# Moving the first of four merges to an earlier tick in a hand-ordered attention-layer kernel

## The reference, cut to what matters

```python
outs, lses = [], []
for g, (win, dil) in enumerate(zip(DSW_WINDOWS, DSW_DILATIONS)):
    sl = slice(g * DSW_HEADS_PER_GROUP, (g + 1) * DSW_HEADS_PER_GROUP)
    o_g, lse_g = dilated_window_attention(qa[:, :, sl], ka[:, :, sl], va[:, :, sl], win, dil)
    outs.append(o_g)
    lses.append(lse_g)
alpha = jax.nn.softmax(jnp.stack(lses), axis=0)
ya = jnp.sum(alpha[..., None] * jnp.stack(outs).astype(jnp.float32), axis=0)
ya = ya.astype(x.dtype).reshape(B, S, DSW_OUT_WIDTH) * jax.nn.silu(za)
pa = ya @ w_proj_a
...
yd = differential_attention(qd, kd, vd, lam)
yd = rms_norm(yd, diff_subln) * (1.0 - lambda_init)
yd = yd.reshape(B, S, DIFF_V_WIDTH) * jax.nn.silu(zd)
pb = yd @ w_proj_b
ga, gb = jnp.split(jax.nn.sigmoid(gm), 2, axis=-1)
y = (ga * pa + gb * pb) @ w_out
```

## Time and profile before

| | |
|---|---|
| time, three executions | 837.82, 837.94, 839.5 us (median 837.94) |
| profiled execution, first to last instruction (the only time shown of it) | 835.3 us |
| TensorE matmul busy | 791.2 us, 95% |
| VectorE, ScalarE, GpSimd busy | 462.2, 360.6, 464.1 us |
| mean granted TensorE clock | 0.979 of full speed |

### The profile page before, as it was taken

The page is one execution under the profiler, slowest core; times in us unless marked ns, Lnnn a source line. Parts: engine busy times, 40 slices in busy tenths (PEclk is TensorE's granted clock), DMA queues, the critical chain, the costliest instruction groups (busy, mean ns, idle before and its releaser), DMA issues.

```text
span 835.3 us, 12656 instructions
## 1 busy us (share of the span) xinstructions
PE 791.2 (95%) x4590; PEld 663.8 (79%) x4590; DVE 462.2 (55%) x715; ACT 360.6 (43%) x777; POOL 464.1 (56%) x616
## 2 busy tenths in 40 slices
PE   3989899998899999999979998998999999999997
PEld 2867798887688888888768787777887778888897
DVE  5855653647646363334686597678666653113632
ACT  6455445533354544434434545455466442323310
POOL 4742545546566573458485586779266276637200
PEclk9889999998999999999989999999999999999999
DMA  9943323385233333243522332243112123324431
GB/s 320 338 141 110 109 73 95 96 284 158 92 97 93 120 101 102 85 143 102 145 75 77 99 92 90 77 123 95 51 63 70 46 75 102 102 76 144 159 102 51
DMA packets 87076, 95.39 MB, mean 114 GB/s; under 512 B 9405, under 2 KB 78310, under 8 KB 87014
## 3 DMA queue, kind: packets, MB, share of 16 engines
q1 hardware_dynamic: 86944, 94.56, 36.6%
q10 hardware_dynamic: 70, 0.02, 0.0%
HBM read 78.53 MB, written 5.54 MB: 101 GB/s over the span
## 4 chain that ended last, share of the span: by engine, by line
PE 67%; DVE 14%; issue 7%; ACT 4%; POOL 3%; DMA 3%; SPq 2%; DVEq 0%; POOLq 0%; ACTq 0%
PE proj L1731 48%; PE proj L1850 4%; PE sums L1654 3%; PE turned L1622 2%; DVE dstat L1346 2%; POOL w_lo L787 2%; PE score L1604 2%; PE score L1570 2%; PE proj L1780 2%; PE sums L1656 2%; ACT probs L1031 2%; DMA rope_s<-rope_x 1%; DVE dstat L1362 1%; DVE at_lo L1369 1%; ACT junk L1063 1%
## 5 line engine op out<-in xcount | busy, mean ns | idle before, releaser
L787 POOL TENSOR_TENSOR w_lo<-raw,w_hi 128x256 fp32r<-128x256 f32 x376 | 299.7, 829 | 209.3 <-ACT w_hi L907 209.3
L1731 PE MATMUL proj<-h_hi,w_hi 128*128 128x512 f32 x560 | 231.5, 413 | 0.0
L1731 PE MATMUL proj<-h_hi,w_lo 128*128 128x512 f32 x560 | 221.6, 396 | 0.0
L1731 PE MATMUL proj<-h_lo,w_hi 128*128 128x512 f32 x560 | 220.1, 393 | 0.0
L1731 PEld LDWEIGHTS proj<-h_hi,w_hi 128*128 128x128 f32 x560 | 106.6, 190 | 30.3 <-issue 8.9
L1731 PEld LDWEIGHTS proj<-h_hi,w_lo 128*128 128x128 f32 x560 | 106.2, 190 | 24.0
L1731 PEld LDWEIGHTS proj<-h_lo,w_hi 128*128 128x128 f32 x560 | 106.9, 191 | 19.9 <-issue 0.5
L907 ACT ACTIVATE w_hi<-raw 128x1024 fp32r<-128x1024 f32 x96 | 100.3, 1054 | 10.4 <-PE proj L1731 7.7
L815 POOL TENSOR_TENSOR rope_x<-rope_x,cos_t 128x512 f32<-128x512 f32 x36 | 56.8, 1579 | 74.0 <-DMA rope_s<-rope_x 73.9
L1369 DVE TENSOR_TENSOR at_lo<-turned,at_hi 128x512 fp32r<-128x512 f32 x64 | 44.0, 688 | 59.7 <-ACT at_hi L1049 59.1
L1031 ACT ACTIVATE probs<-score,dstat 128x512 f32<-128x512 f32 x64 | 43.5, 685 | 59.5 <-DVE dstat L1346 59.5
(11 more groups left out here) (284 smaller groups left out, 1517.0 us busy)
## 6 DMA issues: line engine op xcount, KB each, us to landing
raw<-in_w_in SPq DMA_DIRECT2D x85, 512.0 KB, 3.6
rope_s<-rope_x SPq DMA_DIRECT2D x144, 64.0 KB, 2.1
ada<-in_w_ada SPq DMA_DIRECT2D x24, 256.0 KB, 7.1
zd<-in_w_ada SPq DMA_DIRECT2D x8, 512.0 KB, 6.1
raw<-in_w_proj_b SPq DMA_DIRECT2D x8, 512.0 KB, 3.4
raw<-in_w_out SPq DMA_DIRECT2D x8, 512.0 KB, 3.5
rows_in<-window_rows SPq DMA_DIRECT2D x4, 792.0 KB, 5.0
window_rows<-rows_out SPq DMA_DIRECT2D x4, 528.0 KB, 3.7
```

The costliest lines, as they stand in the source:

```text
L787: nc.gpsimd.tensor_tensor(lo[:, k, :], raw_place(n)[:, k, :], hi.bitcast(F32)[:, k, :], ALU.subtract).then_inc(w_lo_done, 1)
L1731: ins = mm(dst, left, right, start=k == 0 and n == 0, stop=k == nk - 1 and n == 2, skip_group_check=tile.b == 2)
```

## The change

Two tables of ticks are edited. `mix_tick` was 100, 116, 124 and 132 and becomes 88, 116, 124 and 132 (T0[6] is 72 and T0[7] is 96), so only the first merge moves, with the weights of all four. Its turn on TensorE moves from tick 104 to tick 92. The scaling and the turn of the last differential head move by one tick, from 162 and 163 to 163 and 164.

```diff
-    scale_at = by_tick(diff_ends, lambda s: s.pv + (3 if s is not diff_ends[-1] else 2))
+    scale_at = by_tick(diff_ends, lambda s: s.pv + 3)
...
-    y_at = by_tick(diff_ends, lambda s: free_turn(s.pv + (4 if s is not diff_ends[-1] else 3)))
-    mix_tick = [T0[7] + 4 + at for at in (0, 16, 24, 32)]
+    y_at = by_tick(diff_ends, lambda s: free_turn(s.pv + 4))
+    mix_tick = [T0[6] + 16, T0[7] + 20, T0[7] + 28, T0[7] + 36]
```

## The result

| | before | after |
|---|---|---|
| median of 20 runs each, us | 837.76 | 843.62 |
| profiled execution, span, us | 835.3 | 837.8 |
| its mean granted clock of TensorE | 0.979 | 0.977 |

The kernel is slower: the ratio after to before is 1.0064, with a 95% interval of 1.0043 to 1.0085, which is 3.6 to 7.1 us. The runs after lie between 838.9 and 848.1, those before between 834.0 and 844.9, but for one of 1445.33 that stands far outside all others and moves no median. The profiled execution after is one of the quickest (its time is 839.6), so that the two profiles differ by 2.5 us only, and the medians by 5.9. The experiments show what the profile pair misses.

The account below looks back on a forecast made before the run. TensorE, computing 95% of the span, was taken as the bound. Old place -7.6, wait +9.0, clock +3.0 and last head -0.9 sum to +3.5 us: span 835.3 to 838.8, plus 2.6 gives 841.4 us; range 837.8 to 844.6.

Parts of the forecast that it names:

- The wait at the turn: At the first merge's new turn, TensorE idles from 383.8 until the merge ends at 392.8: +9.0 us.
- the chain that I worked out: Ahead of the new turn: swap lets GpSimd's cosine start at 381.5, low-part slices end at 386.2, merge ends at 392.8.
- The clock: Behind the long idle at the new turn, TensorE runs at 1.2 GHz for a while: +3.0 us, ends 1.7 and 3.4.
- The old place: In the ticks the first merge leaves, a 2.94 us stall, its slow clock and a gating wait go: -7.6 us.
- The last head: A 1.43 us wait for scaling goes, new waits of about 0.3 and 0.2 us come: -0.9 us.
- The base: The profiled span of 835.3 us, with 2.6 us added to reach the median of the runs, 837.94.
- (a): Rival at the new turn: early merge, clock near 2.4 GHz, gain pays for the wait; about 837.4 us; chance 0.15.
- (b): Rival at the new turn: merge nearly in time, under 3.8 us of waiting, kernel faster at 833.2 us; chance 0.08.
- the bound of 3.8 us: At the new turn: if the merge is done before 387.6, TensorE waits under 3.8 us and perhaps keeps its clock.
- (c): Rival at ticks 96 to 104: GpSimd's delay makes TensorE wait for weights; 843.4 us if slack is exceeded by 2; chance 0.10.
- The rule taken from the Trainium skill: At the new place, VectorE and GpSimd exclude each other; merge weights ready at 386.5 instead of 383.6, time 841.7 us.

Follow-up runs that it names:

- e1: The changed kernel run again, unedited; 843.81 us, 1.0069 of the kernel before.
- e2: The changed kernel with the last head's scaling and turn put back as before, so only the merge edit remains; 843.46 us, 1.0070 of the kernel before.
- e9: The changed kernel with the first merge's five loads issued behind the second k tile's swap instead of ahead of it; 844.04 us, 1.0070 of the kernel before.
- e4: The changed kernel with the first merge's turn and gating on TensorE at tick 95 instead of 92; 833.23 us, 0.9943 of the kernel before.
- e5: The changed kernel with the first merge back at tick 100 and only the merge weights, their exponential and loads at tick 88; 832.52 us, 0.9940 of before.
- e10: The changed kernel with 46 products of unused result ahead of the first merge's turn, to keep TensorE busy; 841.37 us, 1.0042 of the kernel before.
- e11: The changed kernel with the first merge's turn at tick 95 and its loads behind the swap; 834.10 us, 0.9951 of the kernel before.
- e3: The changed kernel with the merges put back as before, so only the last head's edit remains; 837.49 us, 0.9987 of the kernel before.
- e6: The changed kernel with the first merge's turn and gating on TensorE at tick 94 instead of 92; 838.49 us, 1.0003 of the kernel before.
- e7: The changed kernel with 36 products of unused result ahead of the first merge's turn, to keep TensorE busy; 842.75 us, 1.0059 of the kernel before.

## Why the prediction was right, and where its terms were off

The time forecast was 841.4 us, slower, and the range 837.8 to 844.6. It is 843.62, slower, inside the range, 2.2 us above the forecast. The mechanism held. On the scale of spans +3.5 us was forecast and +5.1 is the mean over profiles, and of the 1.6 between them the old place makes 1.7 and all other terms -0.1. Point by point:

**The wait at the turn, +9.0**, was +9.45 in the profile after and 9.30, 9.26 and 9.40 in e1, e2 and e9. The mechanism is shown, not only argued: with the turn three ticks later the wait and the loss go (e4), with the merge back at tick 100 they go too (e5). Both links of the chain that I worked out (swap until 380.9, merge from 385.35) held to 0.9 us; the merge after took 7.08 where 6.6 was put in, close to the slowest of the earlier trace rows.

**The clock, +3.0**, was mis-sized: it cost 1.9 to 2.7. The low clock was there as said (0.50 from 393 to 396), but I priced it with a stretch of 5.9 us at 1.2 GHz, and here the level rose again some 4 us after work began, and 5.7 in e1. Wait and clock together were forecast at +12.0. Measured are +12.1 with the turn itself, which the sum leaves out at both places, so 11.7 without its 0.4; two errors nearly cancelled, and that was luck.

**The old place, -7.6**, is the term that was off. The stretches lost 7.0 us in the profile pair and 6.3 in the mean over profiles; the turn's own 0.4, which -7.6 leaves out, is in both, so like for like it was -6.6 and -5.9. Two things failed. "What would be late next in these ticks is nothing I can see" is the step: I had looked at the first stalled step and not at the ones behind it. Ticks 106 to 108 took 1.0 us longer in the change, with 0.64 us of idle on `at_lo`. VectorE after, in the timeline ahead of it:

```profile
443.14 0.18 DVE L1407 RECIPROCAL ystat<-ystat 128x4 f32<-128x4 f32 x1
443.23 1.08 DVE L1302 TENSOR_TENSOR k_lo<-rope_o,k_hi 128x512 fp32r<-128x512 f32 x1
444.24 0.68 DVE L1282 TENSOR_TENSOR rope_s<-rope_s,sin_t 128x512 f32<-128x512 f32 x1
445.88 0.42 DVE L1314 TENSOR_TENSOR v<-proj,v 128x256 fp32r<-128x256 f32 x1 [0.96 <-ACT v L1006]
446.37 0.69 DVE L1369 TENSOR_TENSOR at_lo<-turned,at_hi 128x512 fp32r<-128x512 f32 x1
```

`at_lo` stands behind the norm of a head, two rope operations and a v tile that waited for ScalarE. In the kernel before, the gating wait of 1.5 us two ticks earlier gave VectorE the time for all this. But its absence alone doesn't make the stall: e4, e10 and e11 have neither the gating wait nor the stall (8.45, 8.18 and 8.40 us for these ticks). The timelines of after and then of e10 show where VectorE lost the time, at a product of probabilities ahead of that norm:

```profile
439.25 1.29 POOL L815 TENSOR_TENSOR rope_x<-rope_x,cos_t 128x512 f32<-128x512 f32 x1
439.34 1.75 DVE L1363 SCALAR_TENSOR_TENSOR probs<-probs,dstat 128x512 f32<-128x512 f32 x1
```

```profile
440.63 0.75 DVE L1363 SCALAR_TENSOR_TENSOR probs<-probs,dstat 128x512 f32<-128x512 f32 x1
441.74 1.29 POOL L815 TENSOR_TENSOR rope_x<-rope_x,cos_t 128x512 f32<-128x512 f32 x1 [1.16 <-DMA rope_s<-rope_x]
```

Counted from the scores of tick 106, L1363 starts at the same place in both. In after GpSimd's cosine began just ahead of it and it took 1.75 us; in e10 the cosine came behind it and it took 0.75. The norm (L1407) then starts 0.71 us behind these scores in after and 0.62 ahead of them in e10, and through ScalarE's squares and v `at_lo` comes 3.93 and 2.61 us behind them. In the kernel before L1363 took 1.75 us too, and the gating wait made up for it. So, as far as these profiles show, the stall needs both, no gating wait and a VectorE operation drawn out beside GpSimd. Which of the two orders an execution takes was read in these traces and not set by an edit. The second thing is a size from one profile: the stall with its clock spell cost 5.92 in the profile before and 4.49 in e3.

**The last head, -0.9**, was -0.7 in the mean: -0.8 in nine profiles (172.9 to 173.0 against 173.8), and -0.2 in after and e6. The forecast waits of 0.3 and 0.2 us were one of 0.20 in e3 and two in after, this one and 0.21 behind it:

```profile
689.82 0.47 PE L1731 MATMUL proj<-yd_late_hi,w_hi 128*128 128x512 f32 x1 [0.74 <-DVE yd_late_lo L1531]
```

The two operations of L1531 took 2.42 us there and 1.82 in e3. By time the part is unresolved.

**The base.** The sum was made on one execution's span. A run's time is 1.8 us above its span (839.6 and 837.8 after), so the profiled execution before was 0.7 us quicker than the median, and the one after 4.0. The profiled pair moved by +2.5, the means of the terms add up to +5.1 and the medians moved by +5.9. The same code ahead of tick 88 varies by 4 us here, so a difference of two single spans tells less than that.

**Rivals.** (a), that the gain pays for it, needed a wait of 6.8 us and a kept clock; neither came. (b), a merge nearly in time, did not happen. e4 makes the case, with 0.65 us of waiting and 833.23 us, but the bound of 3.8 us was too generous: e6 waits 2.28 us, loses 1.7 more to the clock and 1.6 to low weight parts, and comes out even. (c), weights late for tick 96, didn't come: no wait on low parts stands between the turn and the scores at 403.31. The rule taken from the Trainium skill, SBUF — State Buffer, section "Who interferes with whom", gave 386.5 for the merge's weights. The trace has them at 383.6, where the forecast without the rule put them: the fourteen operations took 6.0 us from 377.60 on and not 5.4. The largest share is L1441's, beside GpSimd's cosine and low parts:

```profile
381.45 2.17 DVE L1441 TENSOR_TENSOR mstat<-mstat 128x32 f32<-128x32 f32 x3
```

They were through ahead of GpSimd's own work, so that by way of the weights the rule had no part in the time. Its mechanism is there all the same, as the last section shows; how much VectorE's operations drew out GpSimd's part of the chain (7.08 us for the merge, against 5.95 at the quickest before) no run separates.

## What to carry to other kernels

An operation can be moved early at no cost only if the place where the bound engine asks for it moves no further than the operation does, plus what it had to spare. Here GpSimd merged 34 us sooner (L848 at 385.35 for 419.25), TensorE asked 51 us sooner (at 383.1, where its turn stood at 433.7), and the merge had had 7.5 us to spare (through at 426.2): 50.6 - 33.9 - 7.5 = 9.2 us is nearly all of the 9.45 waited. The turn three ticks on made a gain of 0.6% out of a loss of 0.6%. Before removing a stall, look at the waits just behind it too: the slack that it gave the other engines goes with it. And price a change of this size from several executions, cut at fixed places of the program, not from the difference of two spans.

## What the runs showed of the hardware

**An idle time doesn't decide by its length alone whether the clock falls.** In e7 2.04 us of idling were followed by 0.50, although TensorE had worked 8.3 us without a break before. In the kernel before, TensorE waited 2.50 us near 578 (at the last merge's gating), and kept 2.4 GHz:

```profile
578.68 0.66 PE L1622 MATMUL turned<-ident,probs 128*128 128x128 f32 x4 [2.50 <-DVE za L1448]
```

```profile
579.00:583.00 4.00, 4.00 (x33) 3.43 (x31) 3.17 (x6) 2.01 (x8) 3.02 (x13) 1.00 0.42 131
```

The same instruction with the same wait in front of it goes both ways. In e1 it waited 2.51 us until 586.83, in e2 2.49 us until 584.27. The clock behind it, first of e1 and then of e2:

```profile
588.00:592.00 4.00, 4.00 (x35) 3.69 (x32) 2.85 (x4) 2.08 (x7) 3.11 (x12) 1.00 0.36 120
```

```profile
586.00:589.00 3.00, 3.00 (x15) 3.00 (x15) 2.75 (x4) 1.11 (x3) 2.26 (x10) 0.50 0.37 129
```

In e2 ticks 138 to 140 took 9.69 us, in e1 8.19. And the longest idle time, 9.45 us, cost less in clock (2.0 us) than 2.94 us did in the kernel before (2.95).

**Small VectorE operations beside GpSimd.** The three 128x32 operations of L1441 took 2.46 us in e1 and 2.17 in after, beside GpSimd's cosine and low parts. In e7, where GpSimd stood still until 384.34, they took 0.40:

```profile
383.91 0.40 DVE L1441 TENSOR_TENSOR mstat<-mstat 128x32 f32<-128x32 f32 x3
```

The Trainium skill, SBUF — State Buffer, section "Who interferes with whom", has a VectorE operation with two SBUF inputs and a GpSimd operation that reads SBUF exclude each other, by an exclusive lock; these rows agree, at 0.7 to 0.8 us on average for an operation that takes 0.13 alone.
